# Attention on one core: values one unit behind the scores, the sums' product opens the low accumulator, next scores ahead of the last maxima

## What is computed

```python
def one_block(qblk):
    s = jnp.einsum('bqhd,bkhd->bhqk', qblk, k, preferred_element_type=jnp.float32) * scale
    p = jax.nn.softmax(s, axis=-1)
    return jnp.einsum('bhqk,bkhd->bqhd', p.astype(v.dtype), v)
```

## Time and profile before

| | |
|---|---|
| median of 3 runs | 3456.26 us (3455.32 to 3460.83) |
| the profiled execution | 3457.05 us, span 3455.3 us |
| TensorE busy over the span | 3244.4 us (94%) |
| VectorE, ScalarE, GpSimd busy | 2024.7, 1707.5, 1398.5 us |
| one steady head in `attention` | 99.88 us |

### The profile page before, as it was taken

One profiled execution on the slowest core, in us unless ns is written; L12 is line 12 of the kernel. 1 busy time (PEld: TensorE's weight loads), 2 busy tenths in 40 slices (PEclk: granted clock), 3 DMA queues, 4 the chain that ended last, 5 costly groups with the idle time before them and its releaser, 6 DMA issues. The chain is left out here.

```text
span 3455.3 us, 46901 instructions
## 1 busy us (share of the span) xinstructions
PE 3244.4 (94%) x17548; PEld 2752.9 (80%) x17548; DVE 2024.7 (59%) x2857; ACT 1707.5 (49%) x2472; POOL 1398.5 (40%) x910
## 2 busy tenths in 40 slices
PE   7979979999999999999979997998999979999899
PEld 6978856777777777777769997786788869999787
DVE  4548878888888888888753333444333234333432
ACT  4436645777777777777744544102222225444200
POOL 1228856888888888888910000000110000000000
PEclk9989979999999999999989998998999989999999
DMA  7858983333213333321053233885323233322565
GB/s 285 307 211 311 328 281 73 63 68 64 50 41 63 68 65 68 64 59 36 11 200 110 89 111 89 243 229 185 140 97 108 81 144 126 107 91 85 165 192 157
DMA packets 380229, 454.75 MB, mean 132 GB/s; under 512 B 51704, under 2 KB 317304, under 8 KB 367728
## 3 DMA queue, kind: packets, MB, share of 16 engines
q1 hardware_dynamic: 380016, 451.91, 42.5%
HBM read 262.07 MB, written 189.64 MB: 131 GB/s over the span
## 5 line engine op out<-in xcount | busy, mean ns | idle before, releaser
L1277 POOL TENSOR_TENSOR at_acc<-at_acc,at_ph 128x1024 f32<-128x1024 f32 x288 | 690.6, 2398 | 76.1 <-ACT at_ph L1203 55.7
L1203 ACT ACTIVATE at_ph<-at_sc 128x1024 fp32r<-128x1024 f32 x408 | 418.5, 1026 | 322.8 <-PE at_sc L1123 322.8
L1311 DVE TENSOR_TENSOR at_pl<-at_sc,at_ph 128x1024 fp32r<-128x1024 f32 x408 | 498.5, 1222 | 129.7 <-ACT at_sc L1204 129.3
L1297 DVE TENSOR_REDUCE at_mx<-at_mxp 128x1 f32<-128x512 f32 x816 | 522.1, 681 | 25.8 <-PE at_mxp L1134 23.8
L1204 ACT ACTIVATE at_sc<-at_sc 128x1024 f32<-128x1024 f32 x408 | 416.0, 1020 | 0.0
L171 PE MATMUL gm_gate<-gm_h,gm_g_hi 128*128 128x256 f32 x1280 | 367.7, 287 | 6.4 <-DVE gm_g_lo L160 6.4
L172 PE MATMUL gm_gate<-gm_h,gm_g_hi 128*128 128x256 f32 x1280 | 362.1, 283 | 0.0
L173 PE MATMUL gm_gate<-gm_h,gm_g_lo 128*128 128x256 f32 x1280 | 361.9, 283 | 0.0
L1119 PE MATMUL at_sc<-at_qt,at_kt 97*128 97x512 f32 x816 | 330.5, 405 | 3.9 <-DVE at_pl L1311 1.9
L1121 PE MATMUL at_sc<-at_qt,at_kt 96*128 96x512 f32 x816 | 325.0, 398 | 0.0
L1148 PE MATMUL at_o_hi<-at_ph,at_v 128*128 128x512 f32 x816 | 322.3, 395 | 2.1 <-DVE at_half L1316 2.1
(11 more groups left out here) (240 smaller groups left out, 7297.1 us busy)
## 6 DMA issues: line engine op xcount, KB each, us to landing
gm_h<-hT SPq DMA_DIRECT2D x48, 1024.0 KB, 7.2
hT<-lat_n_h SPq DMA_DIRECT2D x28, 1024.0 KB, 7.2
qT<-hd_stq SPq DMA_DIRECT2D x60, 384.0 KB, 5.4
kT<-hd_stk SPq DMA_DIRECT2D x60, 384.0 KB, 4.7
at_qt<-qT SPq DMA_DIRECT2D x120, 192.0 KB, 3.0
sgT<-gm_sg SPq DMA_DIRECT2D x80, 256.0 KB, 2.1
ou_o<-omix SPq DMA_DIRECT2D x40, 512.0 KB, 6.3
ou_sg<-sgT SPq DMA_DIRECT2D x40, 512.0 KB, 7.4
```

The costliest lines, as they stand in the source:

```text
L1203: act.activation(ph[:, g], sc[g % 2][:], ACT.Exp, scale=SCALE).then_inc(p_hi, 1)
L1277: pool.tensor_tensor(acc[:, c.slot, :], f32(ph[:, (g - 1) % 4]).rearrange("p b n -> p (b n)") if t == 1 else acc[:, c.slot, :], now, ALU.a ...
L1297: dve.tensor_reduce(mx[:, n:n + 1], mxp[n % 2][:], AX.X, ALU.max).then_inc(mx_in, 1)
L1311: dve.tensor_tensor(pl[:, g], sc[g % 2][:], f32(ph[:, g]), ALU.subtract).then_inc(p_lo, 1)
```

## The change

```diff
+        def total_at(c):
+            return 2 if before(c, 1).sample else 1
...
                         m = pe.matmul(o_lo[0:ROW_HI + 1, :], v[:, c.kv, n, VL:VR], pl[:, g, b, :],
-                                      start=first and b == 0, stop=last and b == 1)
+                                      start=first and b == 0 and not has_before(c), stop=last and b == 1)
...
                 def total(c, alone=False):
                     pe.wait_ge(tot_lo_in, c.n + 1)
+                    pe.wait_ge(low_in, c.n + 1)
...
-                                      start=alone and n == 0, stop=alone and n == 1)
+                                      start=n == 0, stop=alone and n == 1)
...
                 def finish_values(c):
-                    value(c, c.pairs - 2)
-                    if c.pairs == 2 and has_before(c):
-                        total(before(c, 1))
-                    value(c, c.pairs - 1)
+                    for t in range(0 if c.sample else c.pairs - 1, c.pairs):
+                        value(c, t)
...
                         if t < c.pairs - 1:
                             scores(c, t + 1)
+                        elif nxt.exists():
+                            scores(nxt, 0)
                         maximum(*max_pieces(c, t))
-                        if nxt.exists() and t == c.pairs - 1:
-                            scores(nxt, 0)
                         if t == 0 and has_before(c):
                             finish_values(prev)
-                        if t >= 2:
-                            value(c, t - 2)
-                        if t == 3 and has_before(c):
+                        if has_before(c) and t == total_at(c):
                             total(prev)
+                        if not c.sample and t == 2:
+                            value(c, 0)
+                        if not c.sample and t >= 2:
+                            value(c, t - 1)
...
                 last = Chunk(Chunk.COUNT - 1)
                 finish_values(last)
-                pe.wait_ge(low_in, last.n + 1)
                 total(last, alone=True)
...
                 def upper(c):
                     act.wait_ge(valued, c.g0 + c.pairs)
                     after(act, half_in, c.n)
-                    act.copy(up[:], o_hi[VH:2 * VH, :]).then_inc(up_in, 1)
...
                     act.copy(low[:, c.slot, :], o_lo[0:ROW_HI + 1, :]).then_inc(low_in, 1)
+                    act.copy(up[:], o_hi[VH:2 * VH, :]).then_inc(up_in, 1)
...
-                        if has_before(c) and t == (2 if c.pairs == 8 else 1):
+                        if has_before(c) and t == total_at(c) - 1:
                             total_hi(prev)
...
                         if t == 0 and has_before(c):
                             fold(prev)
+                        if has_before(c) and t == total_at(c):
+                            total_lo(prev)
                         if t > 0:
...
-                        if has_before(c) and t == (2 if c.pairs == 8 else 1):
-                            total_lo(prev)
```

## The result

The changed kernel takes 3487.54 us (median of 4, 3486.43 to 3489.36); the kernel before, on the same chip, 3456.11 (3455.32 to 3460.83). The ratio is 1.0086, 95% interval 1.0073 to 1.0098: slower by 31.4 us, where +21 was forecast. The profiled execution's span is 3486.1 us, 30.8 more than before.

The account below looks back on a forecast made before the run. TensorE, busy 99.51 of a head's 99.88 us, was taken as the bound. Terms -31.2 (old waits, stage end), +39.0 and +13.8 (stalls behind `neg`) sum to +21.6 us: 3477 us, own range 3466 to 3488, eight in ten 3447 to 3492.

Parts of the forecast that it names:

- Both old waits: TensorE: S4's wait for `pl`, 0.30 us, and the wait between the maxima at t=7, 0.35 us, both go.
- its cover: T' now waits for `low`; exponentials and M leave 0.5 us to spare, so the added wait costs 0.
- The 58 stalls: Scores wait for `pl` behind a `neg` held by GpSimd's addition: 47 times 0.83 us, 11 times 1.25 us.
- The forecast of a head: A head of the changed kernel, stalls included, takes 101 to 102 us.
- the wait-free head: A head without the old waits or new stalls takes 97.3 us.
- P1 and P2 at t=4: `neg` meets GpSimd's add 5, so S7 waits for `pl`: 0.83 us each.
- The row of the next head's P0: Row DMA of `neg` just fits ahead of S0n, no cost; landing 0.3 us later would cost 14 us.
- slower still: Rival: the row of `neg` lands late as well, adding 14 us, 3491 us; chance 0.10.
- P0 at t=4: Add 5 starts only 0.3 us ahead of `neg`; S7 stalls 1.25 us, 11 times, 13.8 us.
- t=6: In P2 and P3 `neg` meets add 7, so scores wait for `pl`: 0.83 us each.
- The end of the stage: The total goes in front of TensorE's wait for `halves`: 1 us gained, between 0 and 2.07.
- P0 free: Rival: `neg` 0.3 us earlier or the add 0.3 later, no P0 stalls, 3463 us; chance 0.12.

Follow-up runs that it names:

- experiment 1: Changed kernel with the negation of the maxima as a one-element tensor_reduce with negated result instead of a tensor_scalar: 3432.95 us, ratio to before 0.9928.
- experiment 3: Changed kernel with the real negation as a tensor_reduce, plus a spare tensor_scalar behind it writing a tile nobody reads: 3493.93 us, ratio to before 1.0105.
- experiment 5: Changed kernel with every join on GpSimd preceded by a second one into a spare tile, 60 more operations: 3476.8 us, ratio to before 1.006.
- experiment 6: Changed kernel with the total back at t=2 in every chunk behind a prompt chunk: 3508.55 us, ratio to before 1.0154.
- experiment 8: Changed kernel with the negation as tensor_reduce and, in the last chunk only, ScalarE's total rounding behind the second exponentials: 3427.92 us, ratio to before 0.9912.

## Why the prediction was right

**The mechanism, point by point.** Both old waits went (experiment 1 has neither). T' has its cover: no wait for `low` in a steady head of the changed kernel. (It does wait in P3 of the last head, where no maxima are left to cover it: its first matmul starts 0.47 us late.) GpSimd moved up to its inputs: in P1 it waits for `ph` at adds 2, 6 and 7 (the prediction had add 5 among them). Its addition was under way whenever `neg` wanted to start. The 58 stalls are 58. The forecast of a head, 101.8 us, is met by 102.1, and the wait-free head, 97.3, by 97.2 to 97.7. That the form of the negation is the cause is shown by experiments 1 and 3 together, that the addition's timing decides by experiment 5.

The rule of the skill that the prediction named says more on the cure (the Trainium skill, "SBUF — State Buffer", section "Who interferes with whom"): on this chip `tensor_scalar` can enter a two-port mode and contend with GpSimd, `tensor_reduce` never can. Experiment 1 agrees, 157 ns at every place. So does experiment 6 with first come, first served: where the addition was first by 0.35 us, the negation lasted until it ended, 2.10 us. In experiment 5 a negation that was first by 0.12 took 0.17 us, as that rule has it. That the negation enters such a mode is the page's account; the runs show the waiting, and that the form decides it.

**The sizes.** The sum was +21.6 us, the span grew by 30.8; the median of 3487.54 lies only just inside the forecast's own range, 3466 to 3488. A head grew by 2.31 us (fold to fold, 99.83 to 102.14 over the last ten), where the sum says 1.97. Hardly any error went the other way, so the sum was not right by cancelling. The terms, and which were mis-sized:

- *P1 and P2 at t=4*: 0.98 us each instead of 0.83. I let add 5 start with its input, 14.33 after S1, though the chain of additions in front of it was worked out as 14.2 and so was nearly as late. That chain is 0.3 late from add 2 on. In the P2 shown above, whose S1 starts at 990.09, add 2 starts at 5.80 instead of about 5.5, add 4 at 11.95 instead of 11.7, and add 5 at 14.49, behind its input; `neg` ends and S7 starts 0.16 later with it. 24 times that is 4 us.
- *The row of the next head's P0*: nothing, as forecast ("it just fits"), in ten heads of eleven. The scores start 4.04 to 4.07 us behind the first row DMA, one usual step behind the values:

```profile
832.56 2.41 SPq L1055 DMA_DIRECT2D at_qt<-at_neg  x4
```
```profile
836.38 0.40 PE L1154 MATMUL at_o_lo<-at_pl,at_v 128*97 128x512 f32 x1
836.62 0.40 PE L1123 MATMUL at_sc<-at_qt,at_kt 97*128 97x512 f32 x1
```

  In the one other head, the one of 102.40, they start 4.24 behind it (row from 934.67, scores at 938.91): the step is 0.43 and the one behind it 0.34, 0.30 us in all. Experiments 1 and 5 have one such head each, though the row leaves 0.7 us earlier there; a single row that lands late does it, and it is no cost of every head. The rival "slower still" cost 0.3 us once, not 14.
- *P0 at t=4*: 1.21 to 1.27 us, forecast 1.25. *t=6*: 0.84, forecast 0.83. Both as they should be.
- *The end of the stage*: I gave it -1 us. From the end of the last scores to the last copy it takes 14.5 us, before 13.2: +1.3, so 2.3 off. ScalarE rounds the total in front of the last exponentials and waits for the fold of the chunk before, so they start 1.93 us behind the last scores instead of 0.20. Experiment 8 takes that away and ends in 13.1. So even without it the 1 us for the total in front isn't there; no run shows that term. (Experiment 1 still has the wait. Its 14.0 is shorter by the clock alone: granted 0.87 instead of 0.50 over the last 2 us, its last two matmuls step by 0.31 instead of 0.54.)
- *Outside the stage*: 0.8 us ahead of it and 0.9 behind it, in code that is the same in both kernels.

The five stalls of a head come to 4.87 us where the sum has 4.57, and that is nearly all of the 0.34 by which a head is over its forecast; away from the stalls the matmuls step by 0.2327 us, as before. With heads 3.7, end 2.3 and outside 1.7, 7.7 of the 9.2 us are placed. Of the other 1.5, half is in the first chunk and half in the last head, T' of its last P3 among it.

The prediction's rival "P0 free" hung on 0.3 us, and the margin in the trace is 0.31 to 0.35 in ten of eleven heads (add from 650.41, `neg` from 650.76 in the first of them). It was worked out as 20.8 and 21.1 behind S1 of the sample, and measured 20.89 and 21.25, so this was not luck.

## What to carry to other kernels

A wait that costs nothing is a wait whose end isn't late yet: the negation took 744 ns in the kernel before, where it needs 170 with nothing beside it, and only the order around it decided whether that cost 0 or 5 us a head. Before moving an engine up, look at every instruction that lasts longer than its like, ask what it is waiting for, and put that into the new timetable. And where one instruction of a queue is the only one that collides, change its form; moving it or delaying the other side gave back less here (13 and 11 us against 55).

## What was unexpected of the hardware

A `tensor_scalar` of 4 columns from SBUF to SBUF took up to 2.12 us beside a `tensor_tensor` on GpSimd, ending 0.03 us behind it each of 59 times, and a `tensor_reduce` over the same four numbers 0.157 us at all 60 places. And more work made the changed kernel faster: 60 more joins on GpSimd took 11 us off.
